# Hybrid decoder step: where TensorE computes the attention values of a pair of heads

## The chip, the cores and the metric

One core of a Trainium2 chip runs the whole step in one launch. The metric is device time in microseconds (us) of a launch; the kernel before has a median of 1375.18 us over 3 runs.

## What is computed

Two trunk layers of a decoder for 512 prompt tokens and 8 sample tokens (with 1024 cached positions each), all in float32. The change concerns the stick-breaking attention of layer 0 for the prompt, with 8 heads of 64:

```python
z = einsum('bqhd,bkhd->bhqk', q, k) * (SB_HEAD_DIM ** -0.5) + bias
log_stay = where(causal, log_sigmoid(-z), 0.0)
between = cumsum(log_stay, axis=3, reverse=True) - log_stay
weight = where(causal, exp(log_sigmoid(z) + between), 0.0)
out = einsum('bhqk,bkhd->bqhd', weight, v)
```

Around it stand the input projection (q, k, v and a pooling input u), causal pooling, the output projection, two mixtures of 16 experts (group top-1, then top-2 inside it), a convolution module in layer 1, and gated per-layer embeddings. The sample tokens attend to their cached keys and values.

## The kernel before

Each engine has its own instruction stream, written out in the order in which it runs; between streams there are only semaphores. The functions below are small steps of a stream, called in a loop over p = 0 to 3, the four pairs of heads (2p, 2p+1). For a prompt head, keys lie on partitions and queries on columns, in four key blocks whose causal parts are 512, 384, 256 and 128 columns wide, 1280 in all.

A head goes through these steps:

- TensorE, `first_scores(p)` and `last_scores(p)` (line 2007 is the matmul of both): the products of keys and queries of both heads of a pair, in two portions, into PSUM.
- ScalarE, `first_logits(p)` and `last_logits(p)`, three copies each (line 986): scores times scale plus bias, from PSUM to one of four logit buffers (`logits_of(h)`, two in `arena`, two in `xnT`; head h uses buffer h % 4). Each copy raises `s_zs`. From head 4 on, the first copy of a head waits for `s_pv`, that is for the values of the pair that used the buffer before.
- VectorE, `minus_abs(h)` (line 1455), ScalarE, `softplus(h)` (exp at line 1002, ln at 1003), VectorE, `stick_lengths(h)` (line 1460): the negative of log_stay, in `ex`.
- GpSimd, `later_blocks(h)`: four selects that apply the causal mask (line 737), then two copies and two additions (lines 750 to 753) that sum blocks of later keys; the last raises `s_spm`.
- TensorE, `sticks(h)`: the cumulative sums over keys, as products with a triangle (line 2053) and with ones (line 2056). There is one PSUM area for them, so that it first waits until VectorE has used the sums of the head before (`s_dd`). It also waits for `s_spm`, and, ahead of that wait, runs `turn_sample(h - 2)`.
- VectorE, `attend_back(h)` (line 1465): logits minus those sums; raises `s_dd`.
- ScalarE, `weights(h)` (line 1007): exp. GpSimd, `mask_weights(h)` (line 737 again, on the logit buffer): raises `s_wm`.
- TensorE, `values(p)` (line 2067): weights times v for both heads of a pair into one PSUM bank. It waits for `s_wm` of both heads, and for `s_ot`, the copy of the pair before; it raises `s_pv`.
- VectorE, `attend_out(p)` (line 1470): copies that bank to `xnT`; waits for `s_pv`, raises `s_ot`.

Between these stands the work of the sample tokens: `sample_values(b)` (line 2083: cached values of sample b, loaded by GpSimd's indirect transfers), `sample_out(b)` (VectorE, line 1476) and `turn_sample(b)` (line 2090, products of 8 columns). Behind the loop come the copies at lines 1505 and 1506, the pool projection and the output projection (line 1912).

VectorE's loop has the order `attend_back(2p)`, `minus_abs(2p+2)`, `attend_back(2p+1)`, `sample_out(2p)`, `stick_lengths(2p+2)`, `minus_abs(2p+3)`, `sample_out(2p+1)`, `stick_lengths(2p+3)`, `attend_out(p)`. ScalarE's has `last_logits(p+1)`, `weights(2p)`, `softplus(2p+2)`, `weights(2p+1)`, `softplus(2p+3)`, `first_logits(p+2)`:

```python
def logit_part(h, part):
    if part == "a" and h >= 4:
        act.wait_ge(s_pv, 2 * (h // 2) - 2)

def last_scores(p):
    pe.wait_ge(s_zs, 6 * p + 2)
```

GpSimd's loop has `mask_weights(2p)`, `mask_weights(2p+1)`, `later_blocks(2p+2)`, `later_blocks(2p+3)`. TensorE's is in the functions printed here.

Of the kernel before, what the change touches and what calls it, by code (L numbers as in the profile page):

```python
# [162 lines left out]
def decoder_step(nc, a, out):  # L163

    with ExitStack() as ctx:
# [106 lines left out]
        def logits_of(h):  # L272
            return logit_bufs[h % 4]
# [161 lines left out]
        def fill_wait(pe, name, i):  # L435

            n = JOBS[(name, i)][0]
            if n >= 4:
                _, engine, count = BY_NUMBER[n - 4]
                pe.wait_ge(s_drained[engine], count)  # L440
            return slot(n)
# [1422 lines left out]
        def _(pe):  # L1864
# [144 lines left out]
            def first_scores(p):  # L2009

                if p:
                    pe.wait_ge(s_zs, 6 * p)
                for h in (2 * p, 2 * p + 1):
                    ins = score(h, 0, ps[:, h % 2, :])
                ins.then_inc(s_zf, 1)
                score(2 * p, 2, ps_flat[:, 1024:1280]).then_inc(s_zf, 1)

            def last_scores(p):

                pe.wait_ge(s_zs, 6 * p + 2)  # L2020
                for kb, first, width in ((1, 0, 384), (3, 384, 128)):
                    for h in (2 * p, 2 * p + 1):
                        ins = score(h, kb, ps[:, h % 2, first:first + width])
                ins.then_inc(s_zf, 1)
                pe.wait_ge(s_zs, 6 * p + 3)
                score(2 * p + 1, 2, ps_flat[:, 1280:1536]).then_inc(s_zf, 1)
# [15 lines left out]
            def sticks(h):  # L2042

                if h:
                    pe.wait_ge(s_dd, h)
                if h >= 2:
                    turn_sample(h - 2)
                pe.wait_ge(s_spm, h + 1)
                sp, (near, far) = ex[:, h % 2, :], spare[h % 2]
                behind = (far, near, sp[:, 896:1024])  # L2050
                for kb in range(4):
                    col, width = c0 + at[kb], TP - kb * P
                    ins = mm(ps_flat[:, col:col + width], tri[:], sp[:, at[kb]:at[kb] + width],
                             start=True, stop=(kb == 3), skip_group_check=True)
                    if kb < 3:
                        ins = mm(ps_flat[:, col + P:col + width], ones[:], behind[kb],
                                 start=False, stop=True, skip_group_check=True)
                ins.then_inc(s_cf, 1)

            def values(p):  # L2060
                pe.wait_ge(s_wm, 2 * p + 2)
                if p:
                    pe.wait_ge(s_ot, p)
                for kb in range(4):
                    for h in (2 * p, 2 * p + 1):
                        rows = slice(64 * (h % 2), 64 * (h % 2) + 64)
                        ins = mm(ps[rows, 6, kb * P:TP], v_tok[:, kb, h * DH:(h + 1) * DH],
                                 logits_of(h)[:, at[kb]:at[kb] + TP - kb * P], start=(kb == 0), stop=(kb == 3),
                                 skip_group_check=True)
                ins.then_inc(s_pv, 2)  # L2070

            def sample_values(b):

                n = UNIT[("v", b)]
                unit_wait(pe, n)
                if b:
                    pe.wait_ge(s_vo, b)
                else:
                    pe.wait_ge(s_zw, 2)
                rows = unit(n).rearrange("p (f c) -> p f c", f=KEYS)  # L2080
                for f in range(KEYS):
                    g = 32 * (f % 4)
                    ins = mm(ps[g:g + SBH, 7, :], zz[:, b, f, :], rows[:, f, :], start=(f < 4), stop=(f >= 4))
                ins.then_inc(s_vused, 1)

            def turn_sample(b):
                pe.wait_ge(s_vo, b + 1)
                for j in range(4):
                    col = 2816 + (j * TS + b) * SBH
                    ins = mm(ps_flat[:, col:col + SBH], vo[:, b % 2, j * P:(j + 1) * P], fold[:, 0:SBH], start=True, stop=True)  # L2090
                ins.then_inc(s_turned, 1)
# [2 lines left out]
            pe.wait_ge(s_drained["act"], JOBS[("v", 2)][2])  # L2094
            for p in range(SBH // 2):
                sticks(2 * p)
                if p < 3:
                    last_scores(p + 1)
                if not p:
                    pe.wait_ge(s_drained["act"], JOBS[("v", 1)][2])  # L2100
                    pe.wait_ge(s_zv, 1)
                    mm(ps[:, 7, 0:TS * SBH], after[:], zr[:, :, 0, :], start=True, stop=True
                       ).then_inc(s_cs, 1)
                sticks(2 * p + 1)
                if p == 3:
                    pe.wait_ge(s_dd, SBH)
                sample_values(2 * p)
                if p < 2:
                    first_scores(p + 2)
                if p == 3:  # L2110
                    turn_sample(2 * p)
                sample_values(2 * p + 1)
                values(p)
            turn_sample(SBH - 1)


# [393 lines left out]
```

## Time and profile before

| | |
|---|---|
| median of 3 runs | 1375.18 us (1371.82 to 1379.76) |
| the profiled execution | 1377.77 us |
| its span, first to last instruction | 1376.1 us |
| mean granted TensorE clock | 0.975 |
| TensorE matmul busy | 1292.1 us (94%) |
| VectorE busy | 986.3 us (72%) |
| ScalarE busy | 692.6 us (50%) |
| GpSimd busy | 252.6 us (18%) |

The busy time of an engine is the time in which one of its compute instructions ran; the granted clock is a share of 2.4 GHz, so that 0.5 is 1.2 GHz. The span starts at the first instruction, and all times below are counted from there. Matmuls in float32 leave two records each. The attention loop runs from about 153 to 233 us.

### The profile page before, as it was taken

To read this page: it belongs to the slowest core of one execution; us is meant where nothing else is said; L and a number is where in the kernel's file an instruction comes from. 1 tells how busy PE (TensorE), PEld (TensorE's weight loads), DVE (VectorE), ACT (ScalarE), POOL (GpSimd) and SP (SyncE) were. 2 spreads that over 40 slices of the span, in tenths; PEclk is the share of its full clock that TensorE was granted. 3 is DMA by queue.
4 is the path that set the end of the run, shared out by engine and by line. 5 is a ranking of instruction groups with operands and counts; after the bars stand their busy time and mean duration, and the time that the engine had idled before them with its cause. 6 is when DMAs were issued, how large, how long until landed. Compare 5 with 4: busy or idle time off the path is not lost. (4 is left out here: it accounts for less than half of the span.)

```text
span 1376.1 us, 16373 instructions
## 1 busy us (share of the span) xinstructions
PE 1292.1 (94%) x6333; PEld 1016.5 (74%) x6334; DVE 986.3 (72%) x1008; ACT 692.6 (50%) x635; POOL 252.6 (18%) x259
## 2 busy tenths in 40 slices
PE   6999997998999899998999999999799999999897
PEld 5885454876788688887778884587688878887676
DVE  3699663136989788885755999713898888997654
ACT  4001551134678678773641002524468777876455
POOL 2221453001122132210001001020112332220000
PEclk9999999998999999999999999999899999999998
DMA  9779263036799999987450303023479999997301
GB/s 345 276 263 366 93 258 112 1 128 246 283 375 381 292 377 375 368 325 261 152 211 34 123 0 123 1 69 122 151 292 391 391 311 377 390 374 292 138 1 62
DMA packets 121701, 314.10 MB, mean 228 GB/s; under 512 B 9020, under 2 KB 9680, under 8 KB 119568
## 3 DMA queue, kind: packets, MB, share of 16 engines
q1 hardware_dynamic: 105790, 251.94, 50.4%
q0 software_dynamic: 13616, 56.54, 11.3%
q10 hardware_dynamic: 2234, 4.75, 1.0%
q8 instruction: 44, 0.72, 0.2%
q14 instruction: 17, 0.14, 0.0%
HBM read 304.20 MB, written 26.70 MB: 240 GB/s over the span
## 5 line engine op out<-in xcount | busy, mean ns | idle before, releaser
L1912 PE MATMUL ps<-xnT,ring 128*128 128x260 f32 x1408 | 312.5, 384 | 6.5 <-DMA ring<-in_w_in_ab 4.3
L1912 PEld LDWEIGHTS ps<-xnT,ring 128*128 128x128 f32 x1408 | 268.1, 191 | 49.9 <-DMA ring<-in_w_in_ab 4.5
L2190 PE MATMUL ps<-ring_parts,arena_parts 128*128 128x512 f32 x768 | 301.4, 392 | 0.0
L1627 DVE TENSOR_TENSOR ring_parts<-ring,arena_parts 128x2048 fp32r<-128x2048 f32 x96 | 219.5, 2290 | 35.1 <-ACT arena_parts L1096 34.0
L1627 DVE TENSOR_TENSOR ring_parts<-ring,xnT_parts 128x2048 fp32r<-128x2048 f32 x96 | 218.8, 2290 | 32.9 <-ACT xnT_parts L1096 31.8
L1096 ACT ACTIVATE xnT_parts<-ring 128x2048 fp32r<-128x2048 f32 x96 | 183.3, 1918 | 76.5 <-PE ps L2191 60.3
L1096 ACT ACTIVATE arena_parts<-ring 128x2048 fp32r<-128x2048 f32 x96 | 183.2, 1916 | 72.9 <-PE ps L2191 46.3
L2190 PEld LDWEIGHTS ps<-ring_parts,arena_parts 128*128 128x128 f32 x768 | 145.8, 190 | 29.3
L2189 PE MATMUL ps<-arena_parts 128*128 128x512 f32 x384 | 154.8, 403 | 7.4 <-DVE arena_parts L1653 3.8
L2189 PE MATMUL ps<-xnT_parts,arena_parts 128*128 128x512 f32 x384 | 154.2, 401 | 6.8 <-DVE arena_parts L1631 6.8
L2191 PE MATMUL ps<-xnT_parts,arena_parts 128*128 128x512 f32 x384 | 151.2, 394 | 0.0
L2191 PE MATMUL ps<-arena_parts 128*128 128x512 f32 x384 | 151.1, 394 | 0.0
L802 POOL DMA_INDIRECT y_rows<-arena,tab_i x32 | 62.5, 1952 | 453.9 <-ACT arena L1108 412.7
L797 POOL DMA_INDIRECT arena<-x_rows,tab_i x32 | 78.8, 2462 | 154.2 <-DVE tab_i L1611 139.8
L1803 DVE SCALAR_TENSOR_TENSOR arena<-arena,wdw 128x512 f32<-128x512 f32 x120 | 93.2, 777 | 4.9 <-DVE arena L1829 0.2
L1868 PE MATMUL ps<-ident,arena 128*128 128x128 f32 (+7 forms) x613 | 80.4, 274 | 16.7 <-DMA arena<-in_x_prompt 7.0
L1868 PEld LDWEIGHTS ps<-ident,arena 128*128 128x128 f32 (+7 forms) x613 | 71.1, 141 | 29.0 <-POOL cfix L686 6.7
L929 ACT ACTIVATE sq<-hT 128x520 f32<-128x520 f32 x48 | 30.2, 633 | 121.0 <-DVE hT L1515 84.4
L2189 PEld LDWEIGHTS ps<-xnT_parts,arena_parts 128*128 128x128 f32 x384 | 72.9, 190 | 23.2 <-DVE arena_parts L1631 8.2
L2189 PEld LDWEIGHTS ps<-arena_parts 128*128 128x128 f32 x384 | 72.9, 190 | 22.7 <-issue 4.3
L2191 PEld LDWEIGHTS ps<-arena_parts 128*128 128x128 f32 x384 | 72.6, 189 | 17.1
L2191 PEld LDWEIGHTS ps<-xnT_parts,arena_parts 128*128 128x128 f32 x384 | 72.9, 190 | 16.0
(332 smaller groups left out, 1616.3 us busy)
## 6 DMA issues: line engine op xcount, KB each, us to landing
ring<-in_w_gate_e SPq DMA_DIRECT2D x32, 2048.0 KB, 17.9
ring<-in_w_up_e SPq DMA_DIRECT2D x32, 2048.0 KB, 19.9
ring<-in_w_down_e SPq DMA_DIRECT2D x32, 2048.0 KB, 19.6
ring<-in_w_in_ab SPq DMA_DIRECT2D x4, 2048.0 KB, 42.3
ring<-in_w_ple_gate SPq DMA_DIRECT2D x4, 2048.0 KB, 8.3
ring<-y_rows SPq DMA_DIRECT2D x16, 512.0 KB, 7.4
ring<-in_w_in_c SPq DMA_DIRECT2D x4, 2048.0 KB, 8.5
x_rows<-arena ACTq DMA_DIRECT2D x10, 416.0 KB
```

The source lines that it names most:

```text
L797: pool.indirect_dma_start(xg[:, e % GATHERS, :], None, x_rows[layer], bass.IndirectOffsetOnAxis(ap=tab_i[:, 0, e * BLK:e * BLK + 1], axis= ...
L802: pool.indirect_dma_start(y_rows[layer], bass.IndirectOffsetOnAxis(ap=tab_i[:, 1, e * BLK:e * BLK + 1], axis=0), yo[:, e % 2, :], None, bo ...
L929: nc.scalar.activation(sq[:, k % 2, 0:T], src[:, k, :], ACT.Square).then_inc(s_sq, 1)
L1096: nc.scalar.activation(high[hu0 % 4], unit(n)[:, at:at + HU], ACT.Copy).then_inc(s_hi, 1)
L1627: v.tensor_tensor(w_lo, w, high[hu0 % 4].bitcast(F32), ALU.subtract).then_inc(s_lo, 1)
L1803: link(v.scalar_tensor_tensor(y, x, tap, y, ALU.mult, ALU.add))
L1868: return nc.tensor.transpose(dst, src, ident[0:n, 0:n])
L1912: ins = mm(s[:, half, 0:HALF], w[:, k, :], src[:, k, half * HALF:(half + 1) * HALF], start=(k == 0), stop=(k == n - 1))
L2189: mm(ps[:, bank, :], x, w, start=start, stop=False)
L2190: mm(ps[:, bank, :], x, w_lo, start=False, stop=False)
L2191: return mm(ps[:, bank, :], x_lo, w, start=False, stop=stop)
```

## The change

In TensorE's stream `values(p)` is no longer called at the end of its own step. It is called in the next step, behind the first `sticks` of the next pair and in front of `last_scores`; the values of the last pair are called behind the loop, at the place where they were. The other engines' streams are unchanged.

```diff
             for p in range(SBH // 2):
                 sticks(2 * p)
+                if p:
+                    values(p - 1)
                 if p < 3:
                     last_scores(p + 1)
...
                 if p == 3:
                     turn_sample(2 * p)
                 sample_values(2 * p + 1)
-                values(p)
+            values(3)
             turn_sample(SBH - 1)
```

On TensorE, between the first and the second pair, this is the piece of the order where the values of pair 0 stood. L2083 is `sample_values(1)`, L2090 `turn_sample(0)`, and L2053 with L2056 `sticks(2)`:

```order
 L2083 MATMUL ps<-ring,arena 8x512 x8
-L2067 MATMUL ps<-arena 64x512 x2
-L2067 MATMUL ps<-arena 64x384 x2
-L2067 MATMUL ps<-arena 64x256 x2
-L2067 MATMUL ps<-arena 64x128 x2
 L2090 MATMUL ps<-fold,arena 128x8 x4
 L2053 MATMUL ps<-arena,tri 128x512
```

The eight matmuls are gone from there, and `turn_sample(0)` follows the sample values at once. This is the end of `sticks(2)`, where they stand now; L2007 is `last_scores(2)`:

```order
 L2056 MATMUL ps<-arena,ones 128x128
 L2053 MATMUL ps<-arena,tri 128x128
+L2067 MATMUL ps<-arena 64x512 x2
+L2067 MATMUL ps<-arena 64x384 x2
+L2067 MATMUL ps<-arena 64x256 x2
+L2067 MATMUL ps<-arena 64x128 x2
 L2007 MATMUL ps<-arena 128x384 x2
 L2007 MATMUL ps<-arena 128x128 x2
```

They are now between the sticks and the last scores; for pair 1 it is the same, between `sticks(4)` and `last_scores(3)`. For pair 2, on TensorE behind `sticks(6)`, the order has no last scores; L2090 is `turn_sample(5)` and the L2053 behind it begins `sticks(7)`:

```order
 L2056 MATMUL ps<-arena,ones 128x128
 L2053 MATMUL ps<-arena,tri 128x128
+L2067 MATMUL ps<-arena 64x512 x2
+L2067 MATMUL ps<-arena 64x384 x2
+L2067 MATMUL ps<-arena 64x256 x2
+L2067 MATMUL ps<-arena 64x128 x2
 L2090 MATMUL ps<-fold,arena 128x8 x4
 L2053 MATMUL ps<-arena,tri 128x512
```

The values of pair 2 now stand between the two sticks of pair 3.

## Rows read from the trace of the kernel before

**Rows 1.** Busy time by stretch: us, then each engine (instructions), TensorE clock, DMA share, GB/s

```profile
150.00:232.00 82.00, 72.65 (x416) 38.94 (x414) 41.16 (x41) 36.60 (x41) 38.05 (x92) 0.98 0.52 193
232.00:300.00 68.00, 65.81 (x331) 56.05 (x332) 15.50 (x30) 12.01 (x19) 6.90 (x11) 0.97 0.06 13
```

**Rows 2.** Waits, 145 to 240 us: waiting line, line waited for, us, times, longest

```profile
PE ps L1912 <- DVE xnT L1506: 1.8, 1, 1.8
...
PE ps L2083 <- ACT arena L1039: 1.7, 1, 1.7
...
PE ps L2067 <- POOL arena L737: 1.5, 1, 1.5
...
PE ps L2067 <- POOL xnT L737: 1.0, 1, 1.0
```

**Rows 3.** TensorE in order of time: start, duration in us, instruction [idle before it]

```profile
168.99 2.37 PE L2067 MATMUL ps<-arena 128*64 128x512 f32 x16
171.29 1.06 PE L2090 MATMUL ps<-fold,arena 128*128 128x8 f32 x8
172.20 1.10 PE L2053 MATMUL ps<-arena,tri 128*128 128x512 f32 x2
...
175.84 1.57 PE L2007 MATMUL ps<-arena 64*128 64x384 f32 x10
177.49 1.06 PE L2090 MATMUL ps<-fold,arena 128*128 128x8 f32 x8
...
191.50 1.10 PE L2053 MATMUL ps<-arena,tri 128*128 128x512 f32 x2
```

**Rows 4.** GpSimd in order of time

```profile
171.26 0.72 POOL L753 TENSOR_TENSOR rstd<-arena,rms 128x256 f32<-128x256 f32 x1
...
185.00 3.23 POOL L737 TENSOR_SCALAR_AFFINE_SELECT xnT<-xnT 128x128 f32<-128x128 f32 x4 [3.87 <-ACT xnT L1007]
...
190.30 0.73 POOL L753 TENSOR_TENSOR rstd<-arena,rms 128x256 f32<-128x256 f32 x1
...
199.18 1.03 POOL L737 TENSOR_SCALAR_AFFINE_SELECT arena<-arena 128x128 f32<-128x128 f32 x4 [3.90 <-ACT arena L1007]
...
209.60 0.73 POOL L753 TENSOR_TENSOR rstd<-arena,rms 128x256 f32<-128x256 f32 x1
```

**Rows 5.** ScalarE in order of time

```profile
171.90 1.61 ACT L986 ACTIVATE arena<-ps,sbb 128x512 f32<-128x512 f32 x3
...
190.70 1.63 ACT L986 ACTIVATE xnT<-ps,sbb 128x512 f32<-128x512 f32 x3 [0.42 <-PE ps L2067]
```

**Rows 6.** VectorE in order of time

```profile
184.61 1.48 DVE L1460 SCALAR_TENSOR_TENSOR arena<-arena 128x1280 f32<-128x1280 f32 x1
186.01 1.58 DVE L1455 SCALAR_TENSOR_TENSOR arena<-arena 128x1280 f32<-128x1280 f32 x1
...
211.60 0.68 DVE L1470 COPY xnT<-ps 128x512 f32<-128x512 f32 x1
214.54 1.49 DVE L1465 TENSOR_TENSOR xnT<-xnT,ps 128x1280 f32<-128x1280 f32 x1 [2.26 <-PE ps L2053]
```

**Rows 7.** TensorE in order of time, last pair of heads

```profile
210.80 1.11 PE L2053 MATMUL ps<-arena,tri 128*128 128x512 f32 x2
...
216.08 1.06 PE L2090 MATMUL ps<-fold,arena 128*128 128x8 f32 x8 [1.58 <-DVE xnT L1465]
217.00 1.94 PE L2053 MATMUL ps<-arena,tri 128*128 128x512 f32 x2
...
223.97 1.90 PE L2083 MATMUL ps<-ring,arena 128*8 128x512 f32 x16 [1.58 <-DVE xnT L1465]
```

**Rows 8.** Busy time by stretch, as rows 1; the clock stands behind GpSimd

```profile
217.00:222.00 5.00, 5.00 (x14) 2.88 (x14) 0.00 (x0) 0.33 (x1) 1.03 (x4) 0.66 0.00 0
...
234.00:238.00 4.00, 3.32 (x9) 2.71 (x10) 1.06 (x3) 0.00 (x0) 3.08 (x5) 0.57 0.22 18
112.00:118.00 6.00, 3.69 (x28) 2.67 (x27) 4.36 (x4) 0.59 (x1) 1.97 (x2) 1.00 0.98 352
```

## Prediction

> **What bounds the kernel now.** I first read busy time by stage. TensorE is busy 72.65 of the 82 us of the attention stage and 65.81 of the 68 us behind it [rows 1]: outside attention TensorE is the bound, everything there starts from the attention output, and its first weights have long landed, so what attention loses or gains arrives at the end undiminished. Inside attention, the list of waits names the target of the edit. The values matmuls (line 2067) wait twice for GpSimd's masks, 1.0 us for pair 1 (tile xnT) and 1.5 for pair 2 (tile arena) [rows 2]; the values of pairs 0 and 3 wait for nothing. The most that can be taken out of these waits is 2.5 us.
>
> The question is then what else stands near the critical path. Attention is a loop over four engines: a pair's logits (ScalarE), minus-abs and lengths (VectorE), masks and block sums (GpSimd), sticks (TensorE), subtraction (VectorE). I put each engine's stretch in order of time beside the others'.
>
> **What the change moves.** Nothing is added or removed. The matmuls of values(p), p = 0 to 2, go from in front of sticks(2p+2) to behind it; values(3) stays where it was.
>
> 1. *Can sticks(2) start earlier, now that values(0) is gone from before it?* Values(0) takes 171.29 - 168.99 = 2.30 us, and sticks(2) started at 172.20 [rows 3]. But sticks(2) also waits for GpSimd's block sums of head 2; their last addition runs from 171.26 for 0.72, to 171.98 [rows 4], and nothing that they need depends on values. With a handoff of 0.07, my estimate from the gaps between the rows of different engines, sticks(2) starts at 172.05: of the 2.30 only **0.15** is gained, and TensorE now waits where it computed values.
>
> 2. *Behind sticks(2).* Values(0) adds its **2.30**, all on the path. Then last_scores(2) waits for the logits that first_logits(2) copies out (s_zs), and that copy waits for s_pv, which values(0) raises, since the copy overwrites the buffers that values(0) reads. Before, ScalarE began it at 171.90, when values(0) had been done since 168.99 + 2.37; for pair 3 it already waited 0.42 for values before starting at 190.70 [rows 3, 5]. With values directly in front of last_scores on TensorE, nothing hides the copy any more. Its three activations take 1.61 to 1.63 us; the first two, for which last_scores waits, are the wider ones, some 1.2 together. With three handoffs of 0.07 this is a new wait of **1.4** us in front of line 2007. The subtraction of head 2 also starts late, since attend_out(0) stands ahead of it on VectorE and waits for values(0), but 0.68 + 1.49 = 2.2 [rows 6] lies beside 1.4 of wait and 1.57 of last scores. The old gap of 0.08 (177.49 against 175.84 + 1.57) goes. So sticks(3) comes 2.30 + 1.4 - 0.15 - 0.08 = **3.5** us later.
>
> 3. *Pair 1 to 2.* All that makes head 4 ready hangs on sticks(3) and sample_values(2), and shifts by the same 3.5. Before, the block sums of head 4 ended at 190.30 + 0.73 = 191.03, and sticks(4) started at 191.50 [rows 3, 4]. TensorE thus had only 0.4 of slack there after handoff, and the mask wait of 1.0 in front of values(1) was no extra cost: without it (and without the 2.30) TensorE just comes earlier to a wait for those sums. The shift becomes 3.5 - 0.4, and then 2.30 + 1.4 - 0.1 again: **+3.2**, 6.7 in all. Why the sums are late is also there: four mask selects take 1.03 at 199.18 but 3.23 at 185.00 [rows 4], just while VectorE runs two instructions of 128x1280 with both inputs in SBUF, from 184.61 to 187.59 [rows 6]. The order of neither engine changes, so the pattern moves along as a whole. The Trainium skill (SBUF — State Buffer, Who interferes with whom) says that such a VectorE instruction and a GpSimd one that reads SBUF shut each other out for the whole instruction; the trace agrees.
>
> 4. *Pair 2 to 3.* The block sums of head 6 end at 209.60 + 0.73 = 210.33, sticks(6) started at 210.80: again -0.4. Values(2) adds 2.30. No last scores follow. Before, TensorE idled 1.58 from 214.50 for the subtraction of head 6 [rows 7]; now attend_out(2) stands between values(2) and that subtraction, and both are uncovered, 0.07 + 0.68 + 1.49 = 2.24, so +0.7. That is **+2.6**, 9.3 in all. What follows (sample values, values(3), pool projection) keeps its order. The w_out_ab loads and the last cache rows are released by sample_values, up to 7 us later than now, and are needed 20 us or more behind that: nothing.
>
> 5. *TensorE's clock.* The new waits stand beside turn_sample, matmuls of only 8 columns. Before, such a pair (1.58 idle, then 1.06 of 8-column matmuls) was followed by a fall of the granted clock: 0.66 over 217 to 222, a part of it at the level of 1.2 GHz [rows 8]. The sticks there took 222.39 - 217.00 = 5.39 (their end is 223.97 less the idle of 1.58) against 175.84 - 172.20 = 3.64: 1.75 for one fall [rows 3, 7]. Another (turn_sample, then the 1.8 in front of line 1912) gave 0.57 over 234 to 238; but in 112 to 118, with 3.69 busy of 6.00 and no 8-column work beside the wait, the clock stayed at 1.00 [rows 2, 8]. Afterwards turn_sample stands beside idle of 2.1, 3.1, 3.5 and 2.3 us, at sticks(2), (4), (6) and (7). I take three falls in place of one, 2 x 1.75 = **+3.5**. Bounds: the one that was there goes too (-1.75), or five more come, one for each of six new or longer waits (+8.8).
>
> The Trainium skill (TensorE: Matmul & The Clock Gate, HAM oscillation — how this bites in real kernels) speaks against this change: a gap that comes back in each step of a loop throws the array back to its low clock each time. By it the time would be that of the third rival, 1389.8 or more. The trace so far has falls behind two gaps and none behind the 1.7 in front of sample_values(0) [rows 2].
>
> **Sum.** 9.3 + 3.5 = 12.8. Made against the profiled execution (1377.8 us; its span is 1376.1) that gives 1390.6; it stood 2.6 above the median of 1375.2, so on the median I forecast **1388.0 us**.
>
> **Rivals.**
> - *No further fall*: the waits come, and the clock falls no more often than before. 1375.2 + 9.3 = 1384.5. For it: the gaps of 1.7 and 2.3 us without a fall. Against: the new gaps are longer. Chance 0.27.
> - *The copy of the logits stays hidden*: both waits of 1.4 are missing, and no fall comes. 9.3 - 2.8 = 6.5, 1381.7. Against: the 0.42 that ScalarE waits for values already. Chance 0.08.
> - *The clock falls at each gap*: three to five more falls, 9.3 + 5.3 to 8.8, 1389.8 to 1393.3. Chance 0.11.
> - *Not slower, since the block sums don't hold the sticks*: the place is sticks(2), (4), (6). GpSimd, no longer stopped as at 185.00, has the sums ready when TensorE comes. It decides once they end 2.3 us earlier in relation to sticks(3), about the 3.23 - 1.03 = 2.2 that its selects lose. Then pair 0 costs 2.30 - 2.30 + 1.3, pair 1 -1.0 + 1.3, pair 2 -1.5 + 0.7: +0.8, 1376.0. Against: VectorE's order is unchanged, and it stops GpSimd as before. Chance 0.06.
>
> **How the numbers follow.** A measurement of this kernel can tell about 0.5% (6.9 us) from no change. Forecast 0.45; rivals 0.27, 0.08, 0.11, 0.06; a gain by something unseen 0.03. Within 0.5%: 0.08 + 0.06 = 0.14. Slower by more: 0.83. Faster by more: 0.03. The range goes from 1380.5 (copy hidden, and 1.2 below it for the spread of medians) to 1393.5 (five more falls). It leaves out the last rival and the unseen gain.
>
> **What would show it.** Right: line 2053 waits for GpSimd three times for 2 to 3.5 us, where values waited before; line 2007 waits for ScalarE's line 986 twice for 1.4; line 986 waits for line 2067; sticks(7) starts some 9 us later; there are more stretches at 1.2 GHz from 170 to 240. Wrong: sticks(4) right behind turn_sample(2), no wait in front of line 2007, or a later stage that takes up the shift.

## The result, and the profile after

The kernel after has a median of 1394.22 us (1392.03 to 1397.52, 4 runs), the kernel before one of 1376.91 (1371.82 to 1379.76, 4 runs). The ratio is **1.0112, with a 95% interval of [1.0086, 1.0139]**: slower by about 1.1%, or 15.4 us, between 11.8 and 19.1. The plain difference of the two medians is larger, 17.3; all comparisons below go by the ratios. The forecast was 12.8 slower, 1388.0 us on a median before of 1375.2, with a range from 1380.5 to 1393.5. On that base the ratio gives 1390.6, inside the range; the median after alone stands 0.7 above its upper end.

| | before | after |
|---|---|---|
| profiled execution | 1377.77 us | 1392.03 us |
| its span | 1376.1 us | 1390.2 us |
| attention loop: first sticks to first record of line 1912 behind it | 152.99 to 234.68: 81.7 us | 152.63 to 250.01: 97.4 us |
| from there to the end | 1141.4 us | 1140.2 us |
| TensorE matmul busy | 1292.1 us | 1294.4 us |

The loop grew by 15.7 us and the rest of the program took back 1.2; the start was 0.4 earlier. So the whole difference between these two executions arises in the loop, and the loop's length is what the experiments below are read by. TensorE's waits in the loop of 1 us and more, from the trace of after (waiting line, line waited for, us in total, times, longest):

```profile
PE ps L2053 <- POOL rstd L753: 8.2, 3, 3.3
PE ps L2090 <- DVE xnT L1465: 2.2, 1, 2.2
PE ps L2083 <- ACT arena L1039: 1.7, 1, 1.7
PE ps L2083 <- DVE xnT L1465: 1.6, 1, 1.6
PE ps L2007 <- ACT arena L986: 1.4, 1, 1.4
PE ps L2007 <- ACT xnT L986: 1.4, 1, 1.4
```

Against [rows 2], both waits of line 2067 for the masks are gone, 2.5 us. In their place line 2053 (sticks) waits three times for GpSimd's line 753 (the last addition of the block sums), 8.2 us, and line 2007 (last scores) twice for the copied logits, 2.8. This is TensorE's order of time with the places that answer to [rows 3] and [rows 7]:

```profile
168.63 1.06 PE L2090 MATMUL ps<-fold,arena 128*128 128x8 f32 x8
171.68 1.86 PE L2053 MATMUL ps<-arena,tri 128*128 128x512 f32 x2 [2.00 <-POOL rstd L753]
...
177.03 2.37 PE L2067 MATMUL ps<-arena 128*64 128x512 f32 x16
180.77 1.57 PE L2007 MATMUL ps<-arena 64*128 64x384 f32 x10 [1.37 <-ACT arena L986]
...
195.86 2.07 PE L2053 MATMUL ps<-arena,tri 128*128 128x512 f32 x2 [2.83 <-POOL rstd L753]
...
201.17 2.38 PE L2067 MATMUL ps<-xnT,arena 128*64 128x512 f32 x16
204.91 1.57 PE L2007 MATMUL ps<-arena 64*128 64x384 f32 x10 [1.36 <-ACT xnT L986]
...
220.00 2.07 PE L2053 MATMUL ps<-arena,tri 128*128 128x512 f32 x2 [3.34 <-POOL rstd L753]
...
225.19 2.37 PE L2067 MATMUL ps<-arena 128*64 128x512 f32 x16
229.75 1.71 PE L2090 MATMUL ps<-fold,arena 128*128 128x8 f32 x8 [2.19 <-DVE xnT L1465]
231.31 2.05 PE L2053 MATMUL ps<-arena,tri 128*128 128x512 f32 x2
...
239.30 1.90 PE L2083 MATMUL ps<-ring,arena 128*8 128x512 f32 x16 [1.58 <-DVE xnT L1465]
```

The reader should look at the first two-record line of each sticks: 1.86, 2.07, 2.07 and 2.05 us, where a sticks at full clock has 1.10 [rows 3]. From its start to the values behind it, sticks(2) takes 177.03 - 171.68 = 5.35 instead of 3.64; sticks(4) 5.31, sticks(6) 5.19. Sticks(7) takes 239.30 - 1.58 - 231.31 = 6.41 (3.70 at full clock in the runs below), and the turn_sample ahead of it 1.56 instead of 0.92. The granted clock of these stretches agrees (stretch; TensorE, its weight loads, VectorE, ScalarE, GpSimd busy; clock, DMA share, GB/s):

```profile
171.00:178.00 7.00, 6.32 (x20) 3.46 (x22) 1.49 (x1) 0.63 (x1) 4.81 (x11) 0.76 0.05 12
195.00:201.00 6.00, 5.14 (x14) 3.12 (x14) 2.05 (x1) 0.07 (x1) 3.42 (x10) 0.72 1.05 387
220.00:226.00 6.00, 6.00 (x18) 3.40 (x20) 1.29 (x1) 0.00 (x0) 2.69 (x8) 0.74 0.99 369
229.00:239.00 10.00, 7.97 (x22) 5.30 (x22) 1.93 (x2) 1.27 (x1) 1.02 (x4) 0.66 0.00 0
183.00:187.00 4.00, 4.00 (x21) 2.70 (x25) 1.24 (x2) 3.97 (x5) 1.02 (x4) 1.00 0.98 418
```

Of the two levels, 1.2 and 2.4 GHz, the first four stretches had a part at the lower one. The last line is sticks(3), with no wait for GpSimd ahead of it: clock 1.00, and 3.63 us. What the low clock costs in the loop can thus be taken off: 1.71 + 1.67 + 1.55 at sticks(2), (4), (6), and 0.64 + 2.71 in front of and in sticks(7), together 8.3 us; before it was 5.39 - 3.70 = 1.7. Without it the loop is 80.0 us before and 89.1 after. I call this the loop **at full clock**: +9.1 us. The other 6.6 of the 15.7 are clock. Both figures are of one execution of each kernel.

The three engines that TensorE waits for did what [rows 4], [rows 5] and [rows 6] showed, later. Of ScalarE, VectorE and GpSimd in the trace of after:

```profile
179.45 1.63 ACT L986 ACTIVATE arena<-ps,sbb 128x512 f32<-128x512 f32 x3 [7.82 <-PE ps L2067]
...
203.59 1.63 ACT L986 ACTIVATE xnT<-ps,sbb 128x512 f32<-128x512 f32 x3 [8.52 <-PE ps L2067]
```

```profile
189.40 1.48 DVE L1460 SCALAR_TENSOR_TENSOR arena<-arena 128x1280 f32<-128x1280 f32 x1
190.79 1.58 DVE L1455 SCALAR_TENSOR_TENSOR arena<-arena 128x1280 f32<-128x1280 f32 x1
...
227.61 0.69 DVE L1470 COPY xnT<-ps 128x512 f32<-128x512 f32 x1 [6.33 <-PE ps L2067]
228.22 1.48 DVE L1465 TENSOR_TENSOR xnT<-xnT,ps 128x1280 f32<-128x1280 f32 x1
```

```profile
170.90 0.73 POOL L753 TENSOR_TENSOR rstd<-arena,rms 128x256 f32<-128x256 f32 x1
...
189.78 3.23 POOL L737 TENSOR_SCALAR_AFFINE_SELECT xnT<-xnT 128x128 f32<-128x128 f32 x4 [3.94 <-ACT xnT L1007]
...
195.08 0.72 POOL L753 TENSOR_TENSOR rstd<-arena,rms 128x256 f32<-128x256 f32 x1
...
219.22 0.72 POOL L753 TENSOR_TENSOR rstd<-arena,rms 128x256 f32<-128x256 f32 x1
```

Each `x3` copy of the logits begins when values end (177.03 + 2.37 = 179.40), and the second copy's end releases last scores at 180.77. The selects at 189.78 take 3.23 us again, beside the same two VectorE instructions.

### The profile page after: what moved, and what is told of

The parts are those of the page before. It is cut to its first block and busy times, and to the rows that moved or that the text cites. A ratio compares the mean times of both kernels' runs of the same rounds, so it can differ in the third digit from the quotient of the medians.

```text
span 1390.2 us, 16373 instructions
## 1 busy us (share of the span) xinstructions
PE 1294.4 (93%) x6333; PEld 1015.3 (73%) x6334; DVE 985.1 (71%) x1008; ACT 692.3 (50%) x635; POOL 253.5 (18%) x259
## 5 line engine op out<-in xcount | busy, mean ns | idle before, releaser
L1096 ACT ACTIVATE arena_parts<-ring 128x2048 fp32r<-128x2048 f32 x96 | 182.9, 1916 | 77.9 <-PE ps L2193 44.7
L2193 PEld LDWEIGHTS ps<-xnT_parts,arena_parts 128*128 128x128 f32 x384 | 72.1, 188 | 15.7
```

The costliest lines, as they stand in the source:

```text
L1096: nc.scalar.activation(high[hu0 % 4], unit(n)[:, at:at + HU], ACT.Copy).then_inc(s_hi, 1)
L2193: return mm(ps[:, bank, :], x_lo, w, start=False, stop=stop)
```

## The experiments

All were timed beside the kernel before; the ratio is that of all executions, the other columns come from one profiled execution each. "Full clock" is the loop of the profiled execution less what sticks and turn_sample took beyond 3.65 (3.70 for sticks(7)) and 0.92 us.

| run | ratio to before [95%] | loop | clock's part | full clock, against 80.0 |
|---|---|---|---|---|
| after | 1.0112 [1.0086, 1.0139] | 97.4 | 8.3 | +9.1 |
| a_busy | 1.0040 [1.0023, 1.0057] | 90.8 | 1.7 | +9.1 |
| a_outlate | 1.0098 [1.0071, 1.0126] | 89.9 | 3.0 | +6.8 |
| m0 | 1.0039 [1.0020, 1.0058] | 85.1 | 1.7 | +3.4 |
| m2 | 1.0029 [1.0012, 1.0046] | 85.9 | 3.4 | +2.5 |
| a_pool | 1.0114 [1.0084, 1.0143] | 101.0 | 13.4 | +7.6 |
| a_five | 1.0099 [1.0067, 1.0132] | 98.6 | 10.5 | +8.1 |
| m2_outlate | 0.9998 [0.9982, 1.0014] | 82.0 | 1.7 | +0.3 |
| b_tuned_busy | 1.0005 [0.9991, 1.0020] | 83.1 | 0 | +3.0 |
| b_reorder_busy | 0.9978 [0.9957, 0.9998] | 77.9 | 0 | -2.1 |
| b_busy7 | 0.9994 [0.9975, 1.0013] | 80.0 | 0 | 0.0 |
| m2_reorder | 0.9988 [0.9967, 1.0009] | 77.9 | 0 | -2.1 |

What lies outside the loop scatters too: in these profiled executions the loop starts at 152.6 to 155.7, and from its end to the end of the program it is 1134.7 (a_pool) to 1145.2 us (m2_reorder). So loop and ratio need not agree to better than some us.

### Is the rest the clock? (a_busy)

```diff
                 if h >= 2:
                     turn_sample(h - 2)
+                if h in (2, 4, 6):
+                    keep_busy(ps[:, 3, 0:256], {2: 4, 4: 6, 6: 7}[h])
                 pe.wait_ge(s_spm, h + 1)
...
+                if p == 3:
+                    pe.wait_ge(s_zs, 24)
+                    keep_busy(ps[:, 0, 0:256], 4)
                 sticks(2 * p + 1)
```

`keep_busy(dst, n)` gives TensorE n matmuls of 256 columns into a piece of PSUM that nobody reads; the wait for `s_zs` makes sure that the logits have been copied out of that bank.

> The changed kernel, with matmuls of 256 columns whose result nobody reads in the gaps: 4, 6 and 7 of them between turn_sample and the wait for the block sums at sticks(2), (4), (6), and 4 in front of sticks(7). Theory (waits plus clock): of the 15.7 us that the loop (start of the first sticks to start of line 1912) grew from 81.7 to 97.4, 9.1 are waits and the rest is sticks at 1.2 GHz (1.7, 1.7, 1.6 and 3.4 at sticks(7) with its turn_sample). With TensorE kept busy the sticks take 3.6 each, the loop 97.4 - 8.4 = 89, and the run comes 8 us below the changed kernel, 7 above the kernel before. Rival (waits alone matter, and the long sticks are something else, such as the transfers that run meanwhile): the loop stays at 97, the sticks stay at 5.3.

TensorE in order of time around sticks(4) and (5) of this run (here line 2055 is the triangle product of sticks, 2069 values, 2092 turn_sample, 1876 the unread matmuls):

```profile
192.95 2.84 PE L1876 MATMUL ps<-wpool,ones 128*128 128x256 f32 x12
195.94 1.13 PE L2055 MATMUL ps<-arena,tri 128*128 128x512 f32 x2
...
199.59 2.37 PE L2069 MATMUL ps<-xnT,arena 128*64 128x512 f32 x16
203.33 1.57 PE L2007 MATMUL ps<-arena 64*128 64x384 f32 x10 [1.37 <-ACT xnT L986]
204.83 1.06 PE L2092 MATMUL ps<-fold,arena 128*128 128x8 f32 x8
205.75 1.94 PE L2055 MATMUL ps<-arena,tri 128*128 128x512 f32 x2
```

Sticks(4) starts when the block sums allow and takes 199.59 - 195.94 = 3.65, and so do sticks(2), (6) and (7). So the long sticks are the clock's, and with the gaps filled it did not fall there. The structure did not move: +9.1 at full clock. One fall came where none was expected, at sticks(5) (its first line 1.94, the whole 5.33), behind nothing but the 1.37 in front of line 2007 and a turn_sample. The loop was therefore 90.8 and not 89. By the ratio the run is 0.40% above before, 5.5 us (3.2 to 7.9): filling the gaps gave back 9.9 of the 15.4. What is left is less than the 9.1 us of waits that this run's own profile shows, so that some of it comes back outside the loop in most executions, or the kernel before loses more to the clock than its one profile has. No run tells which.

### What does attend_out cost? (a_outlate)

```diff
                 attend_back(2 * p)
+                if p:
+                    attend_out(p - 1)
                 if p < 3:
                     minus_abs(2 * p + 2)
...
                 if p < 3:
                     stick_lengths(2 * p + 3)
-                attend_out(p)
+            attend_out(3)
```

> The changed kernel, with attend_out(p) on VectorE moved behind the first subtraction of the next pair. Theory (attend_out in front of the subtraction is uncovered only in the last pair, where no last scores follow): sticks(7) no longer waits 2.2 us, because the subtraction of head 6 runs beside values(2); the waits in front of line 2007 stay at 1.4. Loop shorter by 2.3, and by up to 3.4 more if the clock does not fall before sticks(7): 91.7 to 95.1 against 97.4; the run 2 to 6 us below the changed kernel. Rival (attend_out holds every pair): all three pairs gain about 0.7 to 2.2, the loop 4 to 6 shorter without any change of the clock.

Its waits (line 2055 is the triangle product, 2009 the last scores):

```profile
PE ps L2055 <- POOL rstd L753: 8.2, 3, 3.3
PE ps L2009 <- ACT arena L986: 1.4, 1, 1.4
PE ps L2009 <- ACT xnT L986: 1.4, 1, 1.4
```

The wait of 2.19 in front of sticks(7) is gone, both waits in front of last scores are still 1.4, and the loop at full clock is 2.3 shorter: only the last pair feels attend_out, as expected. The profiled loop was below the range that I had given, 89.9, because here the clock did not fall at sticks(2) either, behind the same 2.00 us of wait as in after. The ratio shows little of it, 1.0098 with an interval that overlaps that of after; the profiled execution was the fastest of this run's six.

### One pair at a time (m0, m2)

```diff
-                if p:
+                if p - 1 in (0,):
                     values(p - 1)
...
                 sample_values(2 * p + 1)
-            values(3)
+                if p not in (0,):
+                    values(p)
```

(m2 has `(2,)` in both places.)

> Only the values of pair 0 are moved; those of pairs 1 and 2 stay where they were. Theory: the cost is additive by pair, and pair 0 costs 2.30 + 1.4 - 0.3 = 3.4 us of waits plus one fall of the clock at sticks(2), 1.7: loop 81.7 + 5.1 = 86.8, the run 5 above the kernel before. Rival (the loss of one pair is taken up by the slack of the next, as the 0.4 before sticks(4)): under 2 us.

> Only the values of pair 2 are moved. Theory: 2.5 us of waits (values 2.30, attend_out and the subtraction uncovered +0.7, less 0.4 that sticks(6) starts earlier), plus a fall of the clock at sticks(6), 1.6, and perhaps a longer one at sticks(7), 1.7: loop 81.7 + 4.1 to 5.8, the run 4 to 6 above the kernel before. Rival (this is the pair whose values waited longest, 1.5, so that moving it gains): 1 us below.

Pair 0 costs 3.4 at full clock and pair 2 costs 2.5; with the 3.2 of the prediction for pair 1 that is 9.1, what all three cost. So no pair's loss is taken up by the next. The 3.2 can be read in the trace of after as well: counted from the first sticks and less the clock's part, sticks(3) starts 3.45 us later than before and sticks(5) 6.63. In m0's profiled execution sticks(2) took 178.24 - 174.59 = 3.65 behind a wait of 2.0 and a turn_sample: no fall there, and the loop is 85.1 where 86.8 was expected.

```profile
174.59 1.12 PE L2053 MATMUL ps<-arena,tri 128*128 128x512 f32 x2 [2.00 <-POOL rstd L753]
...
178.24 2.37 PE L2067 MATMUL ps<-arena 128*64 128x512 f32 x16
```

In m2 the clock fell at sticks(6) and at sticks(7). Moving the very values that had waited longest (1.5 us) made the kernel 0.29% slower: its rival falls.

### Are the block sums the gate? (a_pool)

```diff
-                for h in (2 * p, 2 * p + 1):
-                    mask_weights(h)
-                for h in (2 * p + 2, 2 * p + 3):
-                    if h < SBH:
-                        later_blocks(h)
+                mask_weights(2 * p)
+                if p < 3:
+                    later_blocks(2 * p + 2)
+                mask_weights(2 * p + 1)
+                if p < 3:
+                    later_blocks(2 * p + 3)
```

> The changed kernel, with GpSimd's block sums of the next pair's first head ahead of the mask of this pair's second head (later_blocks(2p+2) before mask_weights(2p+1)). Theory (the sums of GpSimd release sticks(4) and (6)): they end some 1.0 us earlier, the waits in front of sticks(4) and (6) shrink from 2.8 and 3.3 to 1.8 and 2.3, nothing else moves, the structural part of the loop falls from +9.1 to +7.1; with the clock's part, the run 2 below the changed kernel if the clock falls as often. Rival (values behind the sticks now wait for the later mask): a new wait in front of line 2067 and no gain.

Its waits (line 2054 is the triangle product):

```profile
PE ps L2054 <- POOL rstd L753: 6.5, 3, 2.5
PE ps L2091 <- DVE xnT L1466: 2.2, 1, 2.2
```

The waits for the sums fell from 8.2 to 6.5 (2.8 to 2.0 and 3.3 to 2.5), and the loop at full clock from 89.1 to 87.6. Direction and place are right, and no wait came up in front of values; the size is 0.8 for each of two pairs, where I expected 1.0. The time did not follow, 1.0114 [1.0084, 1.0143]. In the profiled execution the low clock took 13.4 us of the loop, 5 more than in after: here sticks(3) (6.42 us) and sticks(5) (5.30) ran low as well. The rest of the program was 5.5 us shorter than in after.

### Are the logit buffers the gate? (a_five)

```diff
+        qk_flat = arena[:, 0:1280]
...
-            return logit_bufs[h % 4]
+            return qk_flat if h == 4 else logit_bufs[{5: 1, 6: 0, 7: 3}.get(h, h % 4)]
...
-                if part == "a" and h >= 4:
-                    act.wait_ge(s_pv, 2 * (h // 2) - 2)
+                if part == "a" and h >= 5:
+                    act.wait_ge(s_pv, 4 if h == 7 else 2)
```

> The changed kernel, with a fifth logit buffer in the space of the q and k of pairs 0 and 1, dead by then: head 4 uses it, heads 5, 6 and 7 those of heads 1, 0 and 3. So first_logits(2) and (3) wait for s_pv only at their second copy. Theory: the waits in front of line 2007 shrink from 1.37 to about 0.8, each by one copy of 0.6; as the block sums hang on the same chain the gain stays: structural +7.9 instead of +9.1, the run 1.2 below the changed kernel at equal clock. Rival (the wait comes from the subtraction behind attend_out, not from the buffers): 1.37 stays.

```profile
PE ps L2008 <- ACT arena L987: 0.8, 1, 0.8
PE ps L2008 <- ACT xnT L987: 0.8, 1, 0.8
```

Two waits of 1.4 became 0.8, each less by one copy. The loop at full clock is 1.0 shorter. So it is the reuse of the buffers, as the prediction put it, that makes values and last scores follow each other through ScalarE. The time can't tell it from after. In the profiled execution, the slowest of four, the clock was low at five of the six sticks from sticks(2) on (10.5 us in the loop), also at sticks(3), which took 5.28 us behind a wait of only 0.79.

### Can moved values fill a wait at all? (m2_outlate)

```diff
                 attend_back(2 * p)
+                if p == 3:
+                    attend_out(2)
...
-                attend_out(p)
+                if p != 2:
+                    attend_out(p)
```

on top of m2.

> Only the values of pair 2 are moved, and attend_out(2) stands behind the subtraction of head 6 on VectorE. Theory: the 2.30 of values now fill the wait of 1.58 in front of sticks(7) and take 0.7 more, sticks(6) starts 0.4 earlier: structural +0.2. The clock falls at sticks(6), 1.6, and no longer at sticks(7), -1.75: the loop 81.6 to 82, the run equal to the kernel before within 0.2%. Rival (moving values can't fill a wait, since the sums hold the sticks anyway): as moving pair 2 alone, +2.5 and more.

0.9998 [0.9982, 1.0014]: no difference from before. The loop, 82.0, is where the theory had it. Its wait for the sums, now only in front of sticks(6) (line 2056):

```profile
PE ps L2056 <- POOL rstd L753: 3.4, 1, 3.4
```

The one wait that moved values can fill is that for the subtraction in front of sticks(7), and only with attend_out out of the way. What they fill there (1.58) they lose at sticks(6), which waits 3.4 for its sums, where the values themselves had waited 1.5 before.

### Less waiting in place of more cover (b_tuned_busy, b_reorder_busy, b_busy7, m2_reorder)

These start from the kernel before. The edit of b_tuned_busy on ScalarE, VectorE and TensorE:

```diff
                 weights(2 * p)
-                if p < 3:
-                    softplus(2 * p + 2)
                 if not p:
                     act.wait_ge(s_za, 2)
                     nc.scalar.activation(flat(zz), flat(zz), ACT.Exp).then_inc(s_zw, 1)
+                if p < 3:
+                    softplus(2 * p + 2)
...
                 attend_back(2 * p)
+                if not p:
+                    sample_weights()
                 if p < 3:
                     minus_abs(2 * p + 2)
-                if not p:
-                    sample_weights()
                 attend_back(2 * p + 1)
+                if p in (1, 2):
+                    stick_lengths(2 * p + 2)
                 sample_out(2 * p)
                 if p < 3:
-                    stick_lengths(2 * p + 2)
+                    if not p:
+                        stick_lengths(2 * p + 2)
                     minus_abs(2 * p + 3)
...
-                pe.wait_ge(s_wm, 2 * p + 2)
                 if p:
                     pe.wait_ge(s_ot, p)
-                for kb in range(4):
-                    for h in (2 * p, 2 * p + 1):
+                for h in (2 * p, 2 * p + 1):
+                    pe.wait_ge(s_wm, h + 1)
+                    for kb in range(4):
...
+                if p == 3:
+                    pe.wait_ge(s_zs, 24)
+                    keep_busy(ps[:, 0, 0:256], 3)
                 sticks(2 * p + 1)
```

> The kernel before, with the waits shortened where they arise instead of covered: ScalarE's exp of the sample weights ahead of softplus(2) (for the wait of 1.74 in front of line 2083); VectorE's stick_lengths(2p+2) ahead of sample_out(2p) for pairs 1 and 2, so that GpSimd is shut out earlier and the masks and block sums end earlier; in values the even head's four products ahead of the wait for the odd head's mask; and 3 unread matmuls of 256 columns in front of sticks(7), in its wait of 1.58. Theory: 2.8 us less of waits and 1.7 less of clock, loop 77.2, the run 4 below the kernel before (0.3%). Rival (the later sample_out holds the next sample_values): waits in front of line 2083 grow by as much, under 1 us of gain.

This missed: 1.0005, and a loop of 83.1 instead of 77.2. Neither theory nor rival explains it; the trace does, with the values (line 2070 here) of pair 2:

```profile
208.42 1.90 PE L2086 MATMUL ps<-ring,arena 128*8 128x512 f32 x16 [1.84 <-DVE arena L1476]
210.25 3.93 PE L2070 MATMUL ps<-arena 128*64 128x512 f32 x16
214.11 1.06 PE L2093 MATMUL ps<-fold,arena 128*128 128x8 f32 x8
```

A call of values takes 3.86 us instead of 2.30, for four calls 6.2 us, about what the loop is over its forecast. Each single record is as long as before (272 to 643 ns in both traces), but the two heads' products, 64 columns each, overlapped only while they alternated. The trace of a_five lists the alternating records of its last values one by one, even head from `arena`, odd head from `xnT`, and they start in pairs (line 2068):

```profile
247.93 0.64 PE L2068 MATMUL ps<-arena 128*64 128x512 f32 x1
247.93 0.64 PE L2068 MATMUL ps<-xnT,arena 128*64 128x512 f32 x1
248.41 0.59 PE L2068 MATMUL ps<-arena 128*64 128x512 f32 x1
248.41 0.59 PE L2068 MATMUL ps<-xnT,arena 128*64 128x512 f32 x1
```

The one wait that the split removed, 1.03 in front of values(0) (the next run has it), was worth less. Taking the split out again:

> The run before this one without its split of values: the kernel before, with ScalarE's sample exp ahead of softplus(2), stick_lengths(2p+2) ahead of sample_out(2p) for pairs 1 and 2, and 3 unread matmuls in front of sticks(7). The split made one call of values 3.86 us instead of 2.30, since the products of the two heads (64 columns each) no longer alternated. Theory: 2.3 us less of waits than before and 1.7 less of clock, loop 77.7, the run 4 below the kernel before (0.3%). Rival (the split was not what cost the 5 us): loop 80 or more, no difference.

**0.9978 [0.9957, 0.9998]**, a median of 1375.65 against 1378.93: 3 us, and the only version here whose interval lies below the kernel before. The loop is 77.9. The four mask selects between the two VectorE instructions (GpSimd in order of time, this run):

```profile
185.46 2.28 POOL L737 TENSOR_SCALAR_AFFINE_SELECT xnT<-xnT 128x128 f32<-128x128 f32 x4 [4.08 <-ACT xnT L1007]
...
189.82 0.73 POOL L753 TENSOR_TENSOR rstd<-arena,rms 128x256 f32<-128x256 f32 x1
```

They lose 1.2 us instead of 2.2, since only the second VectorE instruction, 186.01 to 187.59, now runs beside them, and the waits of values for pairs 1 and 2 are gone, with values where they were, as is the 1.7 in front of sample_values(0). The price: values(0) now wait 1.03, since TensorE comes to them earlier, and sample_values(3) and (5) wait 0.36 and 1.84 for sample_out (0 and 0.9 before).

The two that remain split this gain up. b_busy7 has the unread matmuls alone; m2_reorder has the reordering, and moved values of pair 2 in place of the unread matmuls:

> The kernel before, with 3 unread matmuls of 256 columns in the wait of 1.58 us in front of sticks(7). Theory (the fall there follows from the gap): sticks(7) takes 3.6 instead of 5.4, the loop 79.9, the run 1.7 below the kernel before (0.1%, at the edge of what can be told). Rival (falls come in some runs only): the loop 79.9 too in the profile, but no difference in the median.

> The reordered kernel without the unread matmuls; instead the values of pair 2 stand behind sticks(6), and attend_out(2) behind the subtraction of head 6. Theory: values fill the wait in front of sticks(7), sticks(6) waits 1.8 for the block sums instead of 3.4: loop 81.7 - 2.2 - 1.75 = 77.8, or 79.4 if the clock falls at sticks(6); the run 2 to 4 below the kernel before. Rival (the sums gate by more): as moving pair 2 with the late attend_out, equal to the kernel before.

b_busy7: loop 80.0, sticks(7) 3.71 instead of 5.39, as expected; the time, 0.9994 [0.9975, 1.0013], can't be told from no change. m2_reorder: loop 77.9, the same as b_reorder_busy, with a wait of 1.5 at sticks(6) and no fall there, and 0.9988 [0.9967, 1.0009], not told from before either. So the gain of 0.2% stands on the edge of what these rounds resolve; what is shown is the loop, 2.1 us shorter at full clock.

## Why the prediction was right, and where its size was off

- **What the values' own waits are worth.** Right. They were not the bound: line 2053 took them over at once, three times, as forecast (2.0, 2.83 and 3.34 us against 2.1, 3.1 and 3.5).
- **Step 1, sticks(2) gains 0.15.** Right: it started 0.52 earlier on the clock of the trace, of which 0.36 is the earlier start of the loop: 0.16.
- **Step 2, the wait for the logits.** Right: 1.37 and 1.36 against 1.4, and a_five shows that the buffers cause it. 3.4 measured in m0 against 3.5.
- **Step 3, pair 1, +3.2.** Not run alone; what is left of 9.1 after m0 and m2 is 3.2, and between sticks(3) and sticks(5) of after the delay grows by 6.63 - 3.45 = 3.2. That the sums gate sticks(4) and (6) is shown by a_pool, and that GpSimd's selects lose the same 2.2 beside VectorE by the row at 189.78.
- **Step 4, pair 2, +2.6.** Right: 2.5 in m2. The part of attend_out, which stands between values and the subtraction, is shown by a_outlate, with 2.3 for the whole wait.
- **Sum of the waits.** 9.3 forecast, 9.1 measured, and again 9.1 in a_busy.
- **Step 5, the clock: the term that was mis-sized.** I took three falls in place of one, 2 x 1.75 = 3.5. The profile has a fall at each of the four gaps, and the last reaches over turn_sample and nearly all of sticks(7), worth 3.4 by itself: 6.6 more than before in the loop. The third rival (a fall at each gap) is what happened in this execution, with 9.3 + 5.3 as its lower end, 14.6 against the 15.7 of the loop. The time by itself doesn't decide between it (14.6 to 18.1 slower) and the forecast (12.8), since the measured difference has the interval from 11.8 to 19.1. The row from 112 to 118 [rows 8], which made me hold back, was no good guide. The wait there had no 8-column work beside it, but no run separates that work from the wait, so that it is not shown to be the reason. The Trainium skill (TensorE: Matmul & The Clock Gate, HAM oscillation — how this bites in real kernels) names this danger, a gap in each step of a loop with a return to the low clock each time. In its example the waits are for transfers, and most are longer than the gaps here. The trace of after agrees at all four gaps; in m0 and a_outlate the first gap, just as long, had no fall.
- **What came back.** The rest of the program was 1.2 us shorter. That lies well inside its scatter, 1134.7 to 1145.2 us in the thirteen profiled executions, and needs no cause in the change.
- **The rival on the other side** (sums ready when TensorE comes): its place was right, its condition not met. Only with VectorE's order changed, in b_reorder_busy, do the sums come sooner.

In the profiled executions the difference is thus 9.1 us of waits and 6.6 of clock. The clock's part differs from execution to execution: 1.7 to 13.4 us of the loop in the profiles of a_busy and a_pool; the waits' part was 9.1 in both after and a_busy. For the 15.4 us over all executions the same split is not shown: filling the gaps took 9.9 of them away, and 5.5 were left.

## What to carry to other kernels

A wait that goes when work is moved out from behind it need not be time gained: look at what the next instruction waits for once it comes earlier, and at which buffers and results the moved work releases, for those are now late for everyone else. Here one engine's idle of 2.5 us was slack in a loop over four engines; moving work into the critical stretch of that loop cost its full length, and its dependents' (copy of the logits, attend_out) on top. Count the gaps that a change opens for TensorE's clock as well, with a range, since here they cost about as much as the waits and scattered far more.

## What the runs showed of the hardware

- TensorE's clock did not follow the length of a gap alone. A wait of 2.00 with a turn_sample (8-column matmuls) in front was followed by sticks at low clock in after, a_pool and a_five (5.35, 5.34 and 5.35 us), and by sticks at full clock in a_outlate and m0 (3.66 and 3.65). In a_busy a fall came behind a wait of only 1.37. In a_five sticks(3) ran low behind one of 0.79. A single execution's profile is therefore no measure of the clock's cost; it takes many timed executions.
- With alternating heads, values take 2.30 us; with one head after the other 3.86, for the same 16 records of the same length. Two products of 64 columns each overlap when they follow each other in turn (they start together at 247.93 and at 248.41), and this was worth more than the wait that the split removed. The Trainium skill (TensorEngine Tiling (Array Packing), Key Properties) says that separate tiles of the array can run their matmuls in parallel; the 2.30 agrees, and the 3.86 shows that the order decides whether they do.
- Four of GpSimd's selects took 3.23 us beside two VectorE instructions with both inputs in SBUF, 2.28 where stick_lengths came 1 us earlier behind the subtraction and only the other one ran beside them, and 1.03 with none. TensorE gained by it because it waits for what GpSimd computes behind these selects.
